# Decoder trunk on one core: attention computed by features, two heads at a time, with latent projections and the meta tokens' chain between the pairs

## The reference

```python
proj = jnp.pad(h @ w_in, ((0, 0), (pad, 0), (0, 0)))          # 1024 -> 1440 columns
qa, ka, va, cq, ckv, kr = split_cols(proj, ATTN_SPLITS)       # 512, 128, 128, 384, 256, 32
o_a = swa_sink_attention(...)                                 # 8 heads of 64, 2 key heads, window 128, a sink per head
qh  = (rmsnorm(cq, q_norm) @ w_uq).reshape(B, Lp, 8, 64 + 32) # latent queries
kvh = (rmsnorm(ckv, kv_norm) @ w_ukv).reshape(B, Lp, 8, 64 + 64)
# the last 32 of a query and the shared kr are turned (rotary), then causal attention over all tokens
o = jnp.concatenate([o_a, o_b], axis=-1)[:, pad:]
return o @ w_out
```

```python
idx = jnp.take_along_axis(cand_i..., best_j, axis=-1)
act = jax.nn.gelu(jnp.einsum('thkd,td->thk', expert_u[idx], xb))
out = jnp.einsum('thk,thkd->td', gate * act, expert_v[idx])
```

## Time and profile before

| | |
|---|---|
| median of 3 runs | 1731.95 us (1727.96 to 1732.09) |
| the profiled execution | 1727.52 us, its span 1725.7 us |
| PE busy | 1451.0 us (84%) |
| VectorE, ScalarE, GpSimd busy | 1147.3, 437.1, 545.2 us |
| DMA | 616.71 MB |

### The profile page before, as it was taken

The page is one execution under the profiler, slowest core; times in us unless marked ns, Lnnn a source line. Parts: engine busy times, 40 slices in busy tenths (PEclk is TensorE's granted clock), DMA queues, the critical chain, the costliest instruction groups (busy, mean ns, idle before and its releaser), DMA issues.

```text
span 1725.7 us, 14681 instructions
## 1 busy us (share of the span) xinstructions
PE 1451.0 (84%) x4075; PEld 678.3 (39%) x4075; DVE 1147.3 (66%) x2944; ACT 437.1 (25%) x1161; POOL 545.2 (32%) x583
## 2 busy tenths in 40 slices
PE   7999998988988777979988968977987977877785
PEld 3456535434433333434433623433334433333332
DVE  3344226776677678776696668687887777777764
ACT  1024212222233222332131222322222222222221
POOL 1011013333434433233333333323333434333331
PEclk9999999999999998999999998989899999999999
DMA  4220208999999999999999999999999999999995
GB/s 166 85 98 1 98 23 350 418 423 367 379 426 427 428 427 391 382 375 422 401 427 423 425 424 397 415 425 424 398 423 426 409 427 427 427 426 427 423 424 212
DMA packets 108095, 616.71 MB, mean 357 GB/s; under 512 B 10827, under 2 KB 12363, under 8 KB 40438
## 3 DMA queue, kind: packets, MB, share of 16 engines
q0 software_dynamic: 76032, 553.68, 76.9%
q1 hardware_dynamic: 31990, 62.17, 9.7%
HBM read 614.77 MB, written 1.05 MB: 357 GB/s over the span
## 4 chain that ended last, share of the span: by engine, by line
PE 49%; DMA 29%; DVE 14%; issue 6%; ACT 2%; POOL 0%; SPq 0%; DVEq 0%; POOLq 0%
DMA arena<-peer_uv,idx 29%; PE bank L853 22%; PE bank L645 14%; DVE arena L1566 5%; PE bank L827 3%; PE bank L754 2%; PE bank L748 2%; ACT arena L1160 1%; PE bank L708 1%; PE bank L719 1%; PE bank L802 1%; DVE h L1572 1%; PE bank L634 1%; DVE wgt L1587 1%; DVE pairs L1551 1%
## 5 line engine op out<-in xcount | busy, mean ns | idle before, releaser
L853 PE MATMUL bank<-arena 128*128 128x512 f32 x1944 | 940.0, 632 | 235.3 <-ACT arena L1160 213.6
L1566 DVE CUSTOM_DVE_ANT_0 arena<-arena,bank 128x1024 f32<-128x1024 f32 x528 | 639.2, 1218 | 346.6 <-DMA arena<-peer_uv,idx 341.6
L591 POOL DMA_INDIRECT arena<-peer_uv,idx x528 | 515.7, 977 | 935.7 <-PE bank L853 881.1
L853 PEld LDWEIGHTS bank<-arena 128*128 128x128 f32 x1944 | 375.1, 200 | 754.3 <-issue 728.0
L1160 ACT ACTIVATE arena<-con,wgt 128x128 f32<-128x128 f32 x486 | 170.7, 394 | 726.6 <-DVE wgt L1587 717.8
L645 PE MATMUL bank<-wring,hT 128*128 128x512 f32 (+5 forms) x604 | 258.8, 584 | 0.4 <-ACT hT L1056 0.4
L645 PEld LDWEIGHTS bank<-wring,hT 128*128 128x128 f32 (+1 forms) x604 | 108.1, 181 | 144.5 <-issue 140.8
L1149 ACT ACTIVATE gl<-dots 128x2 f32<-128x2 f32 x264 | 53.6, 203 | 284.0 <-DVE dots L1566 283.4
L1587 DVE SCALAR_TENSOR_TENSOR wgt<-gate_e,z,gl 128x2 f32<-128x2 f32 x264 | 57.5, 218 | 23.9 <-ACT gl L1149 17.7
L1572 DVE SCALAR_TENSOR_TENSOR h<-arena,wgt,h 128x1024 f32<-128x1024 f32 x42 | 53.9, 1284 | 1.5
L562 POOL TENSOR_TENSOR small<-small,con 128x1 f32<-128x1 f32 (+2 forms) x12 | 7.8, 654 | 137.1 <-DVEq L1329 87.4
(11 more groups left out here) (157 smaller groups left out, 920.8 us busy)
## 6 DMA issues: line engine op xcount, KB each, us to landing
wring<-gla_w_in SPq DMA_DIRECT2D x12, 2048.0 KB, 19.7
arena<-peer_uv,idx POOLq DMA_INDIRECT x528, 11.6
wring<-gla_w_out SPq DMA_DIRECT2D x4, 2048.0 KB, 19.9
wring<-peer_w_query SPq DMA_DIRECT2D x4, 2048.0 KB, 19.6
wring<-attn_w_in SPq DMA_DIRECT2D x2, 2048.0 KB, 8.2
wring<-attn_w_out SPq DMA_DIRECT2D x2, 2048.0 KB, 7.9
gws<-peer_w_query SPq DMA_DIRECT2D x2, 2048.0 KB, 10.0
wring<-attn_w_in SPq DMA_DIRECT2D x1, 1664.0 KB, 13.7
```

What stands on the lines that cost most here:

```text
L591: nc.gpsimd.indirect_dma_start(out=uvrow[:, n % RING, :], out_offset=None, in_=io["peer_uv"].rearrange("l e d -> (l e) d"), in_offset=bass ...
L853: last = nc.tensor.matmul(yacc[:, 512 * i:512 * i + 512], wdiag[:, k % DIAGS, :], rows_of(g, k, 1)[:, 512 * i:512 * i + 512], start=first, ...
L1566: v.tensor_tensor_reduce(out=rows, in0=rows, in1=xnow, scale=1.0, scalar=0.0, op0=ALU.mult, op1=ALU.add, accum_out=dots[:, g % 2, k:k + 1] ...
```

## The change

- **By features.** Chunks of `h` itself are turned (`chunk_T`), and the norm is put on when VectorE takes them to `hT` (272 live columns). Projections then give features on the partitions and tokens along the columns: `front_cols` does 8 matmuls of 128x272 for each 128 features. No q or k is turned per head any more.
- **Two heads at a time.** The heads go in 8 pairs. Sliding-window pairs take head x and x+4. The two heads of a pair lie in rows 0 to 63 and 64 to 127 of q and k (scores, banks 0 and 1), and their outputs in rows 0 to 63 and 64 to 127 of bank 5 (values), so that neighbouring matmuls use different halves of the array. Latent heads need a second matmul for the 32 turned features.
- **Probabilities are scaled by GpSimd** (`scale_probs`) before they are turned; outputs go straight to `hT`, so the turns of the output (`tr_o`) are gone.
- **Fill.** Projections from the latents, the rotary turns (a matmul by `swap`, a product by `cos` on GpSimd, two VectorE instructions), the meta tokens' attention (16 queries on 16 keys, 16 heads), their output projection, norm, queries and choice of experts stand in the list `FILL`, between the pairs, through banks 7 and 6 (`front_filled`, `front_emptied`).
- `keep_warm` is gone. GpSimd's first fetch now waits for the last pair (`o_taken`) as well as for `idx_ready`; before, the meta tokens' choice came long after the heads.

The core of the diff (of GLA and PEER nothing else is changed):

```diff
+FILL = {-2: [("turn_k",), ("kn", 0), ("kn", 1), ("kn", 2), ("kn", 3), ("qr", 0), ("qr", 1), ("qn", 0), ("turn_q", 0), ("qn", 1), ("turn_q", 1)],
+        -1: [("qn", 2), ("qn", 3), ("v", 1), ("s_meta", 0), ("s_meta", 1), ("s_meta", 2), ("s_meta", 3), ("v", 2)],
+        0: [("v", 0), ("sk", 0), ("sk", 1), ("pt_meta",)], 1: [("gain", 1, 0), ("o_meta",), ("gain", 1, 1), ("ao_meta", 0)],
+        2: [("ao_meta", 1)], 4: [("tr_meta", 0), ("tr_meta", 1), ("pq_rows", 0)], 5: [("pq_rows", 1), ("pq_T",)], 6: [("score_meta",)]}
+META_EXPS = -1
+FRONT_UNITS = (
+    [("ka",), ("va",), ("cq", 0), ("cq", 1), ("cq", 2), ("cq", 3), ("cq", 4), ("kr",), ("sums",), ("qa", 0), ("qa", 1),
+     ("rs", 0), ("rs", 1), ("qa", 2), ("qa", 3)] + [u for i in sorted(FILL) for u in FILL[i]])
+FRONT_AT = {u: n for n, u in enumerate(FRONT_UNITS)}
+FRONT_BANKS = (7, 6)
+ROPE_ORDER = (0, 2, 1, 3, 4, 6, 5, 7)
...
-        def pipeline(eng, head_step):
-
-
-            head_step(0, 0, 0, (0, 1, 2))
-            for latent in range(2):
-
-                with eng.Fori(3 * latent, 3 * latent + 3) as j:
-                    head_step(2 * j + 1, 1, latent)
-                    head_step(2 * j + 2, 0, latent)
-            head_step(HEADS - 3, 1, 1)
-            head_step(HEADS - 2, 0, 1, (-1, 0, 1))
-            head_step(HEADS - 1, 1, 1, (-1, 0))
-            head_step(HEADS, 0, 1, (-1,))
...
+            def turn_cos(raw, dst):
+
+                nc.gpsimd.tensor_tensor(dst, raw, acst("cos"), ALU.mult).then_inc(cos_ready, 1)
+
+            def scale_probs(n):
+
+                pool.wait_ge(rden_ready, n + 1)
+                for b in (2, 1):
+                    a, w = SCORE_AT[b]
+                    p = prob[:, n % 6, a:a + w]
+                    nc.gpsimd.tensor_scalar(p, p, stat[:, n % 6, 8 + b:9 + b], None, ALU.mult).then_inc(scaled, 1)
+
+            pool.wait_ge(small_in, SMALL_LOADS * 16)
+            wait_front_emptied(pool, ("kr",))
+            turn_cos(rope_in[:, 2], kT_rope)
+            for i in range(2):
+                wait_front_emptied(pool, ("qr", i))
+                turn_cos(rope_in[:, i], qT_rope[:, i])
+            for n in range(HEADS):
+                scale_probs(n)
+                if n == 7:
+                    root(small[:, 0:1], small[:, 3:4], 1)
+            pool.wait_ge(o_taken, PAIRS)
...
+            def front_cols(u, n_k, w, src, parts=P):
+
+                b = front_begin(u)
+                for k in range(n_k):
+                    last = nc.tensor.matmul(bank[0:parts, b * 512:b * 512 + LIVE], w(k), src(k), start=(k == 0), stop=(k == n_k - 1))
+                front_end(last, u)
+
+            def live(k):
+                return hT[:, k, PAD:ROWS]
+
+            def chunk_T(c):
+
+                for b in range(NB):
+                    src = h[:, b, c * P:c * P + P]
+                    a, n = LIVE_AT[b], live_parts(b)
+                    if b:
+                        last = nc.tensor.transpose(bk(c % 7, a, a + n), src, ident)
+                    else:
+                        last = nc.tensor.matmul(bk(c % 7, a, a + n), src, ident[:, PAD:P], start=True, stop=True)
+                last.then_inc(chunk_turned, 1)
...
+            def queries_a(t):
+                w = part(weights("in_qa"), 0, KC, 512)
+                front_cols(("qa", t), KC, lambda k: w[:, k, t * P:t * P + P], live)
+
+            def latent_rs(i):
+                if i == 0:
+                    pe.wait_ge(norm_rs, 2)
+                front_end(spread_rs(12 + 3 * i, front_begin(("rs", i)), small, 0), ("rs", i))
+
+            keys_a()
+            values_a()
+            for i in range(LATENTS):
+                latents(i)
+            key_rope()
+            latent_sums()
+            queries_a(0)
+            queries_a(1)
+            latent_rs(0)
+            latent_rs(1)
+            queries_a(2)
+            queries_a(3)
...
-            def keep_warm():
-
-                nc.tensor.matmul(bk(3), ident, con[:, 0:512], start=True, stop=True)
...
+            def score_swa(out, hh, qs, ks):
+                r = slice(hh // 4 * HD, hh // 4 * HD + HD)
+                return nc.tensor.matmul(out, qT_swa[r, hh % 4, qs], kT_swa[r, ks], start=True, stop=True)
+
+            def score_nope(out, x, qs, ks):
+                r = slice(x % 2 * HD, x % 2 * HD + HD)
+                nc.tensor.matmul(out, qT_nope[r, x // 2, qs], kT_nope[r, x // 2, ks], start=True, stop=False)
+
+            def score_rope(out, x, qs, ks):
+                r = slice(x % 2 * HD + x // 2 % 2 * 2 * ROPE, x % 2 * HD + x // 2 % 2 * 2 * ROPE + 2 * ROPE)
+                return nc.tensor.matmul(out, qT_rope[r, x // 4, qs], kT_rope[r, ks], start=False, stop=True)
...
+            def pair_scores(p):
+
+                if p < HALF // 2:
+                    wait_front_emptied(pe, ("qa", p))
+                if p == HALF // 2:
+                    latent_heads_ready()
+                if p:
+                    pe.wait_ge(masked, 4 * p)
+                for b in (2, 1):
+                    a, w = SCORE_AT[b]
+                    qs, ks = slice(LIVE_AT[b], LIVE_AT[b] + P), slice(0, w)
+                    heads = [(bk(i, a, a + w), ORDER[2 * p + i]) for i in range(2)]
+                    if p < HALF // 2:
+                        done = [score_swa(out, hh, qs, ks) for out, hh in heads]
+                    else:
+                        for out, hh in heads:
+                            score_nope(out, hh - HALF, qs, ks)
+                        done = [score_rope(out, hh - HALF, qs, ks) for out, hh in heads]
+                for last in done:
+                    last.then_inc(scored, 1)
+
+            def transpose_pair(p):
+
+                if p:
+                    pe.wait_ge(pt_high, p)
+                for i in range(2):
+                    n = 2 * p + i
+                    pe.wait_ge(scaled, 2 * n + 2)
+                    if p:
+                        pe.wait_ge(pt_low, n - 1)
+                    for at, (b, kb) in enumerate(KEY_BLOCKS):
+                        a = SCORE_AT[b][0] + LIVE_AT[kb]
+                        nc.tensor.transpose(bk(2 + i, at * P, at * P + P), prob[:, n % 6, a:a + P], ident)
+                    for b in (1,) if p < HALF // 2 else (1, 2):
+                        a, at = SCORE_AT[b][0], 4 * 512 + 2 * P * i + (b - 1) * P
+                        last = nc.tensor.transpose(bank[0:N_META, at:at + P], prob[:, n % 6, a:a + N_META], ident)
+                    last.then_inc(p_transposed, 1)
+
+            def pair_values(p):
+
+                pe.wait_ge(pt_low, 2 * p + 2)
+                pe.wait_ge(pt_high, p + 1)
+                if p == HALF // 2:
+                    for b in range(NB):
+                        wait_front_emptied(pe, ("v", b))
+                if p:
+                    pe.wait_ge(o_taken, p)
+                at = 5 * 512
+                n = P if p < HALF // 2 else 2 * P
+                rows = [bank[i * HD:i * HD + HD, :] for i in range(2)]
+                heads = ORDER[2 * p:2 * p + 2]
+                for i, hh in enumerate(heads):
+                    nc.tensor.matmul(rows[i][:, at:at + 2 * P], values_of(1, hh), probT[:, i, 0:2 * P], start=True, stop=False)
+                for i, hh in enumerate(heads):
+                    nc.tensor.matmul(rows[i][:, at:at + n], values_of(0, hh), probT_meta[0:N_META, i, 0:n], start=False, stop=False)
+                for i, hh in enumerate(heads):
+                    last = nc.tensor.matmul(rows[i][:, at + P:at + 2 * P], values_of(2, hh), probT[:, i, 2 * P:3 * P], start=False, stop=True)
+                last.then_inc(pv_done, 1)
+
+            for i in range(-2, PAIRS + 1):
+                if i + 2 < PAIRS:
+                    pair_scores(i + 2)
+                if i >= 1:
+                    pair_values(i - 1)
+                for u in FILL.get(i, ()):
+                    fill(u)
+                if 0 <= i < PAIRS:
+                    transpose_pair(i)
+            pe.wait_ge(o_taken, PAIRS)
+            for u in FRONT_UNITS[-2:]:
+                wait_front_emptied(pe, u)
+            pe.wait_ge(con_in, 16)
...
+            def mask_scores(n):
+
+                dve.wait_ge(scored, n + 1)
+                if n >= 6:
+                    dve.wait_ge(p_transposed, n - 5)
+                hh = ORDER[n]
+                st, mask = stat[:, n % 6], acst("mask_swa" if hh < HALF else "mask_mla")
+                for b in (2, 1):
+                    a, w = SCORE_AT[b]
+                    v.tensor_tensor_reduce(out=prob[:, n % 6, a:a + w], in0=bk(n % 2, a, a + w), in1=mask[:, a:a + w], scale=1.0, scalar=-3e38,
+                                           op0=ALU.add, op1=ALU.max, accum_out=st[:, b:b + 1]).then_inc(masked, 1)
+                dve.wait_ge(masked, 2 * n + 2)
+                v.tensor_scalar(st[:, 3:5], st[:, 1:3], sink[:, hh:hh + 1], -1.0, ALU.max, ALU.mult).then_inc(nm_ready, 1)
+
+            def denominators(n):
+
+                dve.wait_ge(probs_ready, n + 1)
```

(33 more changed lines are left out.)

892 lines of the change are left out of this document (485 added, 407 removed).

## The result

Four runs of the changed kernel took 1689.6 to 1695.98 us, median 1690.51, beside a median of 1732.02 for the kernel before. The ratio is 0.9766, 95% interval 0.9746 to 0.9786: 41 us gained, where 69 were forecast. The profiled execution took 1689.6 us, its span 1687.8.

What follows compares the result with a forecast made beforehand. Before `pick` PE bounds the kernel, behind ao of block 1 fetches and mixing. PE reaches `pick` at 173.2 us and ao ends at 190.6, not 259.9: 1731.95 - 69.3 = 1662.6 us, range 1642 to 1686.

Steps and rivals of the forecast that it cites:

- The step that failed: Fetch-bound stage behind ao of block 1: no line of it changes, so it stays 1466 us within 5.
- first sign of being wrong: Named beforehand as showing the prediction wrong: a stretch behind ao that changed.
- First scores: Front of the kernel, before the first pair's scores: PE gets there at 63.7 us, where the heads began at 107.
- key tile: In the front, behind the products that make `hT`: it ends just behind them, at 16.1 us.
- The loop of pairs: Iterations i=-2 to 8, from the first scores to `pick`: 106.5 us, and 3 us more for the clock.
- `pick` and ao of block 1: Behind the loop: 1.7 us and 13.75 us, and 1.9 for the clock, ending at 190.6 us instead of 259.9.
- The halves: Pairs' matmuls in two array halves: 0.79 of the serial price, scores 1.1 (latent 2.2), values 1.35 (1.7) us.
- The rival that the halves don't overlap: In the loop, each pair pays the serial price: +7 us, 1669; chance 0.18.
- GpSimd: Scaling of probabilities in the loop: at least 0.65 us a head, hidden behind the pair at up to 2.2.
- The clock: PE's granted clock falls in i=0, i=3 and i=6 to 8: 3 us in the loop, 1.9 for ao.
- whole halves: Case in the loop where two array halves always run at once: 6 us less, given as 1653.
- the one on the stage behind: Rival that fetches cannot start the next tile sooner, so nothing reaches the end: about 1732 us; chance 0.01.

Runs made afterwards that it cites:

- the serial order: The changed kernel with all matmuls of a pair's first head, then all of the second, in scores and values: 1723.25 us in one run.
- the 8 spare columns: The changed kernel with an unused buffer of 8 columns (32 bytes a partition) behind `con`: 1669.04 us, ratio 0.9648.
- the kernel with the spare matmuls: The changed kernel with 8 unused columns and nine spare matmuls into bank 0 where PE waits: 1662.63 us in one run.

## Why the prediction was wrong

The forecast was 1663 us, from 1642 to 1686; the time was 1690.5. Against the profiled execution (1658.2 forecast, 1689.6 measured) the 31.4 us fall on four terms: +25.7, +5.7, -1.2 and +1.2.

- **The step that failed:** "the span from the end of ao of block 1 on as long as before, 1466 us within 5". It was 1491.4, +25.7. I had said that nothing in that stage changes, and looked only at instructions and their order. The place of its buffers changed, by a constant moved from one table to another, and with it the price of a fetch: 1351.9 us of packet time instead of 1327.1 for the same packets. A changed stretch behind ao was the first sign of being wrong that I had named; I had no mechanism for it. With the rings back on a multiple of 256 bytes that stretch took 1467.9 to 1474.2 us in six kernels, 2 to 8 more than before. Why not 1466 stays open: the packet time is 2 to 7 us longer there as well, in every kernel with the new attention, and I have one profiled execution of each.
- **First scores:** 63.7 us forecast, 69.4 measured, +5.7. Five of it are the key tile. I let it end "just behind" `hT`; it starts at 14.94 and takes 6.09 us, where the latent tiles take 3.7. Its first 11 records took 0.45 us each (below), twice the 0.23 of the last five: that is 2.4 us, and the late start the other 2.5. Values, latent tiles and rope key then took 5.62 and 22.00 us, forecast 5.4 and 22.0.
- **The loop of pairs:** 109.5 us with the clock forecast, 108.3 measured. From the starts of the pairs' scores (69.36, 82.42, 93.58, 101.03, 117.83, 129.22, 134.61, 149.02) the iterations i=-2 to i=4 took 13.1, 11.2, 7.5, 16.8, 11.4, 5.4 and 14.4 us, forecast 13.4, 12.6, 8.1, 15.5, 11.4, 5.0 and 14.5. i=5 to i=8 took 28.7, forecast 26.0 without the clock.
- **`pick` and ao of block 1:** 17.4 forecast, 18.6 measured. By the clock ao lost 1.1 us where I had 1.9, and `pick`, which I had left at full rate, lost 2.1.

The key tile of the first scores, in two parts of the chain:

```profile
14.94 4.94 PE bank L770 x11
...
19.88 1.15 PE bank L770 x5
```

I had read half rate off PE's first four records and then took it at full rate from the chunks on. The key tile still ran at half rate until 19.7 us, though the window row gives the clock as 1.00 there.

**The halves.** 1.1 and 2.2 us for the scores and 1.35 and 1.7 for the values were forecast; 0.95, 2.22, 1.31 and 1.53 came. The sizes are right and the reason isn't: not an overlap of a fifth, but a whole one, and on top of it some 0.2 us for each change of the number of rows (by the price by columns, a latent pair's scores would be 1.41 us wholly overlapped). The two errors cancel, which is luck. The prediction had set the parallel halves and the drain at a change of mode against each other, as the two ends of its range; the traces have both. The rival that the halves don't overlap is refuted by the serial order.

**GpSimd** was hidden as forecast, but for 0.7 us in one iteration. I had the sums behind VectorE's wait "for the pair after next"; they are for the next pair, and I didn't ask what else waits behind them.

**The clock** was 0.92 over the loop. It fell in i=6 to 8, as forecast. It did not fall where PE waited in i=0 (1.00 from 96 to 100 us, with PE busy for 2.1 of the 4 us) nor in i=3. It fell ahead of that wait, at the end of i=-1:

```profile
92.00:94.00 2.00, 2.00 (x4) 0.50 (x5) 0.63 (x5) 0.38 (x1) 1.31 (x2) 0.50 0.00 0
```

PE had not waited there: just before, to 90.6 us, it had run the 48 records of the meta tokens' scores, 16 columns each. It fell again in i=1 (0.51 from 105 to 112 us), behind their values, 32 records of 16 rows and columns. That these small matmuls bring the lower clock is likely and not shown: with the 8 spare columns the same 48 records left it at 1.00, and it fell behind the wait of i=0 instead (0.50 from 100 to 102 us). Two errors hide in the sum again: tiny matmuls are cheaper than the 0.11 us I took (48 in 2.65 us, and 32 in 1.04 with the clock up), and the fill behind them is dearer.

Two figures of the prediction don't follow from its own terms: the parts ahead of the first scores add up to 63.5 us, not 63.7, and 1663 less the 6 us of whole halves is 1657, not 1653. Neither changes the outcome.

No rival of mine held the outcome. All but one priced the loop or its clock, and the range's upper end with them, and the one on the stage behind asked only when its fetches start; none asked what the change does to a buffer that it doesn't name. With the rings back in place the time is 1669.0 us for the 1663 forecast, inside the range.

## What to carry to other kernels

When a kernel is bound by DMA, the address of the landing buffer is part of its tuning: print the start of each ring after every change of any table ahead of it, and pad it to a multiple of 256 bytes; here 32 bytes decided over 20 to 25 us of 1690. A step that "nothing changes" is a term like any other: compare its packet time and GB/s per slice first, for they split a slower stage into less work per us and more work. And a piece of the chain is worth no more than its lead over the next chain: ask what the waiting engine would do in that time (4.2 us on the chain here, 0.7 in hand). For matmuls in halves of the array, keep those with the same number of rows together: of the four changes in a latent pair's scores two could go by this order, 0.4 us a pair by the prices above, an estimate that no run here tests.

## What the runs showed of the hardware

- Fetches of 8192 byte rows into on-chip memory reach 427 to 428 GB/s in the page's highest slices when each row lands on a multiple of 256 bytes, and 421 to 422 at 32, 64, 128 or 224 bytes past one; the packets take 1327 to 1334 us in seven kernels and 1346 to 1353 in seven.
- Float32 matmuls in the two halves of the array run entirely side by side (0.66 us for 272 columns of both heads, 0.65 for one head's), and a matmul of the free half starts ahead of records that stand before it in the code, as long as the number of rows stays the same: a window pair's scores took 0.95 us in one order and 0.94 in the other.
- A change of the number of rows, 64 to 32 or back, cost some 0.2 us at 272 and 144 columns and 0.09 at 16. With it between them the heads of a latent pair did not overlap (4.36 us instead of 2.22).
- The granted clock fell during or behind 32 records of 16x16 that followed each other without a gap (1.00 from 102 to 104 us, 0.56 from 104 to 108, in the kernel with the spare matmuls), so filling the waits of i=0 did not hold it there. No run takes these matmuls away, so whether they or the waits ahead of them brought the lower clock is open.
- A multiplication of 128x272 by a factor per partition took GpSimd 1.03 us and one of 128x144 0.69, and two heads' four of them 3.14 us in most places and 4.2 in one.
